# One inference step of a four-layer diffusion trunk: conditioning blocks moved out of the expert stages, permutation gathers, row-half expert blocks

## The reference

```
mod = (silu(cond) @ ada_w[l] + ada_b[l])           # 6 x 1024: shift, scale, gate, twice
h = h + gate1 * mixer(rmsnorm(h) * (1 + scale1) + shift1)
t = rmsnorm(h) * (1 + scale2) + shift2
group = top-1 of 4 by softmax(t @ w_gr + b_gr); experts = top-2 of the group's 4
h = h + gate2 * sum over the two chosen e of w_e * (silu(t @ w_gate[e]) * (t @ w_up[e])) @ w_down[e]
```

## Time and profile before

| what | value |
|---|---|
| median of 3 runs | 1820.84 us (1820.57 to 1822.17) |
| execution that was profiled | 1820.69 us |
| its span, first to last instruction | 1818.9 us |
| TensorE busy | 1723.6 us, 95% |
| VectorE, ScalarE, GpSimd busy | 518.1, 364.6, 99.8 us |
| moved | 614.07 MB, mean 338 GB/s |
| mean granted TensorE clock | 0.973 |

### The profile page before, as it was taken

How to read it: one execution, slowest core, us unless ns; L and a number is a source line. 1 busy time by engine, 2 the same in 40 slices (tenths; PEclk the granted TensorE clock), 3 DMA queues, 4 the chain that set the end, 5 groups by cost and what they waited for, 6 DMA issues and landing times.

```text
span 1818.9 us, 20710 instructions
## 1 busy us (share of the span) xinstructions
PE 1723.6 (95%) x8682; PEld 899.4 (49%) x8682; DVE 518.1 (28%) x1146; ACT 364.6 (20%) x703; POOL 99.8 (5%) x151
## 2 busy tenths in 40 slices
PE   5999999999999999999999999999999999799995
PEld 2554344467545434334864443435786644434441
DVE  1130221220442122130022222215234982312123
ACT  2121010121232101021202210112322651201111
POOL 0000000000000000000000000000002950000000
PEclk8989999999899999999999999999999999899998
DMA  9999999999349999998545999998864576599993
GB/s 401 312 424 426 424 423 425 422 378 346 118 156 427 425 423 426 423 382 342 208 185 208 426 424 426 423 424 318 322 229 153 154 229 235 208 426 424 427 422 132
DMA packets 109073, 614.07 MB, mean 338 GB/s; under 512 B 16721, under 2 KB 16865, under 8 KB 60465
## 3 DMA queue, kind: packets, MB, share of 16 engines
q1 hardware_dynamic: 102032, 585.73, 79.5%
q0 software_dynamic: 6944, 26.96, 4.6%
HBM read 608.34 MB, written 4.33 MB: 337 GB/s over the span
## 4 chain that ended last, share of the span: by engine, by line
PE 82%; DVE 5%; DMA 5%; ACT 2%; issue 2%; SPq 2%; POOL 0%; DVEq 0%; POOLq 0%; ACTq 0%
PE psum L1082 23%; PE psum L604 14%; PE psum L597 12%; PE psum L1116 11%; PE psum L1064 6%; PE psum L1133 5%; PE psum L663 4%; DMA ring<-in_moe_w_up 2%; SPq L422 1%; DMA acc<-in_moe_w_up 1%; DVE arena L1803 1%; PE psum L701 1%; DMA ring<-in_fnet_w_o 1%; PE psum L1102 1%; ACT arena L1414 1%
## 5 line engine op out<-in xcount | busy, mean ns | idle before, releaser
L1082 PE MATMUL psum<-ring,arena 128*64 128x512 f32 x1152 | 343.4, 594 | 3.5 <-DMA acc<-in_moe_w_up 2.0
L597 PE MATMUL psum<-at,ring 128*128 128x256 f32 x1024 | 223.6, 380 | 0.0
L597 PEld LDWEIGHTS psum<-at,ring 128*128 128x128 f32 x1024 | 193.7, 190 | 28.4 <-issue 1.6
L1082 PEld LDWEIGHTS psum<-ring,arena 128*64 128x64 f32 x1152 | 108.5, 137 | 168.4 <-issue 168.4
L1082 PE MATMUL psum<-arena 128*64 128x512 f32 x608 | 190.0, 594 | 0.0
L1875 DVE TENSOR_TENSOR outtmp<-psum,gate 128x512 f32<-128x512 f32 x128 | 87.6, 684 | 323.7 <-PE psum L1133 323.7
L604 PE MATMUL psum<-ring,at 128*128 128x512 f32 (+1 forms) x416 | 173.5, 572 | 0.4 <-DVE at L1718 0.4
L1116 PE MATMUL psum<-ring,arena 128*64 128x512 f32 x624 | 138.6, 593 | 0.0
L1866 DVE TENSOR_TENSOR arena<-arena,psum 128x512 f32<-128x512 f32 x32 | 33.9, 1059 | 360.9 <-PE psum L1082 360.9
L1064 PE MATMUL psum<-arena,xn 128*128 128x128 f32 x1024 | 126.0, 284 | 6.4 <-issue 6.4
L604 PE MATMUL psum<-ring,arena 128*128 128x512 f32 x288 | 128.4, 604 | 3.0 <-DMA ring<-in_fnet_w_o 3.0
(11 more groups left out here) (254 smaller groups left out, 1550.2 us busy)
## 6 DMA issues: line engine op xcount, KB each, us to landing
ring<-in_ada_w SPq DMA_DIRECT2D x43, 2048.0 KB, 12.6
ring<-in_moe_w_down SPq DMA_DIRECT2D x39, 2048.0 KB, 22.7
ring<-in_moe_w_up SPq DMA_DIRECT2D x38, 2048.0 KB, 15.8
ring<-in_moe_w_gate SPq DMA_DIRECT2D x34, 2048.0 KB, 18.0
arena<-in_moe_w_gate SPq DMA_DIRECT2D x22, 2048.0 KB, 14.8
arena<-in_moe_w_down SPq DMA_DIRECT2D x17, 2048.0 KB, 20.0
arena<-in_moe_w_up SPq DMA_DIRECT2D x16, 2048.0 KB, 19.7
ring<-in_ssd_w_in SPq DMA_DIRECT2D x12, 2048.0 KB, 8.9
```

Of the source, the lines that this page charges most:

```text
L597: last = nc.tensor.matmul(dst, slot(k)[:, c, m * P:(m + 1) * P], src[:, c, :], start=(c == 0), stop=(c == nk - 1))
L1082: last = nc.tensor.matmul(ps[b][e * CAP:(e + 1) * CAP, :], rows, slot_half(k + e, 4, h)[:, c, :], start=(h == 0 and c == 0), stop=(h == 1 ...
```

## The change

- **Round 0 of the next layer** leaves the routing stretches. A1.0 is loaded and multiplied at the start of layer 1, A2.0 behind Q4 and Q5, A3.0 behind I7 and I0. Layer 1's own later rounds move one step later.
- **Layer 0** goes stream by stream as the other layers do. O0 and O1 are issued right behind round 0 of the conditioning. Routers and biases come as contiguous rows into a spare tile and VectorE copies them.
- **Gathers.** Pair x now holds experts x and x+8, of different groups, so a token is in at most one of them. For each stream VectorE completes the one-hot matrix to a permutation (`permutations`), and the gather becomes transposes with it, one bank for each stream. ScalarE copies stream 0's bank, VectorE merges stream 1's over it under a mask (`merged`). Pair 0 keeps the products.
- **Blocks.** G and U blocks now hold half of the rows of both experts, as D's did; `pair_rows` waits for one block at a time and frees it after its half.
- **Order in the expert loop.** The turns of the activations lie between the halves of the down product, the two halves of the gather around the scatter.

```diff
-    return rest[:EARLY], {0: rest[EARLY:4], 1: rest[4:6], 2: rest[6:8]}
+    rest, after = ada_names(n, (1, 2)), ada_names(n + 1, (0,)) if n < 3 else []
+    if n == 1:
+        return [], {0: rest[0:2], 1: rest[2:4], 2: rest[4:6], 3: rest[6:8], 4: after[0:2], 5: after[2:4]}
+    return rest[:3], {0: rest[3:4], 1: rest[4:6], 2: rest[6:8], 3: after[0:2], 4: after[2:4]}
+EVICTED = {1: {1: (1, 1), 3: (1, 2)}, 2: {0: (2, 1), 2: (2, 2), 4: (3, 0)}, 3: {0: (3, 1), 2: (3, 2)}}
+TURNED = {1: {2: (1, 1), 4: (1, 2)}, 2: {1: (2, 1), 3: (2, 2), 5: (3, 0)}, 3: {1: (3, 1), 3: (3, 2)}}
...
-    ada_names(0, (0, 1)) + ["O0", "A0.2.0", "A0.2.1", "O1", "A0.2.2", "A0.2.3"] + ada_names(1, (0,)),
-    mixed(1, [f"Q{j}" for j in range(6)]) + ["O0", "O1"] + ada_names(2, (0,)),
-    mixed(2, [f"I{j}" for j in V_FIRST]) + [f"O{j}" for j in range(4)] + ada_names(3, (0,)),
+    ada_names(0, (0, 1)) + ["A0.2.0", "A0.2.1", "A0.2.2", "O0", "A0.2.3", "O1"],
+    ada_names(1, (0,)) + mixed(1, [f"Q{j}" for j in range(6)]) + ["O0", "O1"],
+    mixed(2, [f"I{j}" for j in V_FIRST]) + [f"O{j}" for j in range(4)],
...
+def issued(n):
+    if n == 0:
+        return ada_names(0, (0,)) + ["O0", "O1"] + ada_names(0, (1, 2)) + MOE
+    if n == 1:
+        return MIX[1] + ["U0.0", "U0.1", "G0.0", "G0.1"] + MOE[4:]
+    return MIX[n] + MOE
...
+            first_up = n == 1 and w in ("U0.0", "U0.1")
+            if n == 0 or expert and not first_up:
...
-                if k == AT[0, "O0"]:
-                    sp.dma_start(wr[:, :, :, 0:EG], a["wgr"]).then_inc(consts_in, 16)
...
+                if k == AT[0, "A0.2.0"]:
+                    sp.dma_start(routers[:, 0, 0:128], a["wgr"].rearrange("p l c e -> p (l c e)")).then_inc(consts_in, 16)
...
+                    half = rows.rearrange("p (e x) c n -> p x e c n", e=2)[:, x, :, c * e:c * e + c, :]
+                    if ROOM[k] == RING + 2:
...
+                        load(k, rooms[ROOM[k]].rearrange("p (e c n) -> p e c n", e=2, c=c), half)
...
+            def first_map():
+                map_part(0, 0, 0, 0, ft, 1)
+                ada_slot(0, "A0.2.0")
+                map_part(0, 0, 1, 0, ft, 1)
+                ada_turned(0, 1)
+                ada_slot(0, "A0.2.1")
+                ada_slot(0, "A0.2.2")
+                map_part(0, 1, 0, 0, ft, 1)
+                ada_slot(0, "A0.2.3")
+                stream_turned(0, 1, 0)
+                for half in range(2):
+                    last = dense_tok(AT[0, "O1"], 1, ps[out_bank(0, 1, 1)][:, :], ft, half * DC // 2, DC // 2,
+                                     half == 0, half == 1, wc0=half * DC // 2)
+                    if half == 0:
+                        ada_turned(0, 2)
+                last.then_inc(slot_done, 1)
...
+                    if n == 1:
+                        if s == 0:
+                            ada_slot(1, "A1.0.3")
+                        else:
+                            ada_turned(1, 0)
...
                     ada_turned(0, 0)
+                elif n == 1:
+                    for q in range(3):
+                        ada_slot(1, f"A1.0.{q}")
                 else:
...
@@ -808,6 +823,7 @@
                         for c in range(4):
                             last = nc.tensor.transpose(bank(4 + h, 4, P)[:, c, :], kT[:, 4 * h + c, 0:P], mat("ident"))
                         last.then_inc(kt_mm, 1)
...
+                            pe.wait_ge(mod_ready, 3 * (n + 1) + 1)
                         if i >= 3:
...
-                    stream_logits(n, 0)
-                    stream_logits(n, 1)
-                    stream_folded(n, 0)
-                    stream_folded(n, 1)
-                    stream_tokens(n, 0)
-                    stream_tokens(n, 1)
-                    for q in range(QUARTERS):
-                        ada_slot(n, f"A1.0.{q}")
-                else:
-                    stream_logits(n, 0)
-                    if n < 3:
-                        for q in range(2):
-                            ada_slot(n, f"A{n + 1}.0.{q}")
-                    stream_folded(n, 0)
-                    stream_turned(n, 1, 1)
-                    stream_tokens(n, 0)
-                    stream_logits(n, 1)
-                    stream_folded(n, 1)
-                    stream_tokens(n, 1)
-                    if n < 3:
-                        for q in range(2, QUARTERS):
-                            ada_slot(n, f"A{n + 1}.0.{q}")
...
+                nc.tensor.matmul(of_pos[:, 3, :], mat("ones"), sel16[:, 0, :], start=True, stop=False)
+                nc.tensor.matmul(of_pos[:, 3, :], mat("ones"), sel16[:, 1, :], start=False, stop=True).then_inc(pos_mm, 1)
...
+                def gather(x, t):
+                    pe.wait_ge(onehot_ready, PAIRS * n + x + 1)
                     for s in range(S):
-                        last = nc.tensor.transpose(bank(3, S, P)[:, s, :], onehot_w[:, s, :], mat("ident"))
-                    last.then_inc(gt_mm, 1)
+                        if s:
+                            pe.wait_ge(xg_merged, MERGES * n + 2 * (x - 1) + t)
+                            if x == 1:
+                                pe.wait_ge(xg_ev, 2 * PAIRS * n + 2)
+                        else:
+                            pe.wait_ge(xg_ev, 2 * (PAIRS * n + x) + t)
+                        for cc in range(4):
+                            c = 4 * t + cc
+                            last = nc.tensor.transpose(bank(4 + s, 4, P)[:, cc, :], xn[:, s, c * P:(c + 1) * P], onehot[:, s, :])
+                        last.then_inc(xg_mm, 1)
+                    if t:
...
                 def pair_rows(x, w, b):
-                    k = AT[n, f"{w}{x}.0"]
-                    arrive(k)
-                    arrive(k + 1)
                     for h in range(2):
-                        pe.wait_ge(xg_ev, 2 * (PAIRS * n + x) + h + 1)
+                        k = AT[n, f"{w}{x}.{h}"]
+                        arrive(k)
+                        if x:
+                            pe.wait_ge(xg_merged, MERGES * n + 2 * (x - 1) + h + 1)
...
+                            pe.wait_ge(xg_ev, 2 * PAIRS * n + h + 1)
...
-                def down_product(x):
...
+                        if h and between is not None:
+                            act_transposes(between)
...
-                        down_product(x - 1)
+                        down_product(x - 1, x)
+                        if x < LAST:
+                            gather(x + 1, 0)
+                        scatter(x - 1)
                     else:
-                        if n < 3:
-                            ada_turned(n + 1, 0)
-                        gather(1)
-                    act_transposes(x)
-                    if 0 < x < LAST:
-                        gather(x + 1)
-                    if x:
-                        scatter(x - 1)
+                        gather(1, 0)
+                        act_transposes(0)
+                    if x < LAST:
+                        gather(x + 1, 1)
...
+            def permutations(n):
...
+                kept, count, before = q(0), q(1), q(2)
+                link(V.tensor_scalar(taken[:, 1:S + 1, :], posr[:, S:S + 2, :], float(CAP), None, ALU.min))
+                link(V.tensor_scalar(before, posr[:, 0:S, :], float(CAP), None, ALU.min))
...
+            def merged(n, x, t):
+                if t == 0:
+                    starts = taken[:, 1, :].rearrange("p (e x) -> p e x", e=2)[:, :, x:x + 1].to_broadcast([P, 2, CAP])
+                    link(V.tensor_tensor(of_late[:, :, :], mats[:, MAT_AT["iota"], 0:CAP].unsqueeze(1).to_broadcast([P, 2, CAP]), starts, ALU.is_ge))
+                dve.wait_ge(xg_mm, (GATHERS + 2) * n + 2 + 4 * (x - 1) + 2 * t + 2)
+                dve.wait_ge(xg_ev, 2 * (PAIRS * n + x) + t + 1)
+                V.copy_predicated(xg[:, x % 2, 4 * t:4 * t + 4, :],
+                                  of_late[:, :, :].rearrange("p e j -> p (e j)").unsqueeze(1).to_broadcast([P, 4, P]),
+                                  bank(5, 4, P)).then_inc(xg_merged, 1)
...
                 for x in range(PAIRS):
                     activated(x)
-                    if x == 0 and n < 3:
-                        modulation(n + 1, 0)
+                    if x < LAST:
+                        merged(n, x + 1, 0)
                     if x:
-                        for i in range(4):
+                        for i in range(3):
                             add_rows(x - 1, i)
+                    if x < LAST:
+                        merged(n, x + 1, 1)
+                    if x:
+                        add_rows(x - 1, 3)
                     if x + 2 < PAIRS:
                         build_onehot(n, x + 2)
```

More of the change, by code:

```diff
@@ L93 @@
 LAST = PAIRS - 1
-def first_issued(n):
-    return {0: [], 1: ["A2.0.0", "A2.0.1", "G0.0", "G0.1", "A2.0.2", "A2.0.3"],
-            2: ["G0.0", "G0.1", "A3.0.0", "A3.0.1", "A3.0.2", "A3.0.3"], 3: ["G0.0", "G0.1"]}[n]
-ISSUE = []
-for _n in range(DEPTH):
-    _early = first_issued(_n)
-    for _w in MIX[_n] + MOE:
```

(64 more changed lines are left out.)

213 lines of the change are left out of this document (122 added, 91 removed).

## The result

The changed kernel takes 1831.1 us (median of 5 runs, 1830.12 to 1832.46), the kernel before 1820.84 beside it: ratio 1.0053, 95% interval 1.0042 to 1.0064. It is slower by some 10 us, where the sum forecast no change at 1822 and the stated range ended at 1831. The execution profiled took 1830.44, its span is 1828.7, 9.8 more than before. TensorE is busy 1696.8 us, 26.8 less than before, and the span is longer.

The account below looks back on a forecast made before the run. Transfers were taken to bound the expert stages (TensorE by a hair in layer 3), TensorE the dense ones. Opening -7.7, stages -28.8, entrance +8.4, moved slots +22.3, routing +6.6, waits 0.5 gave +1.3: 1822 us, range 1811 to 1831.

Parts of the forecast that it names:

- forecast case: Whole kernel: all terms as summed, 1822 us, own range 1815 to 1829; chance 50%.
- rival 3: Layer 1's entrance: Q0 lands later than 28.5 after the last down block, clock low; 8 us more, 1830; 20%.
- named signs of being wrong: Stages of 213 or more, products waiting on VectorE, first Q product over 31 after last landing, TensorE gaps between Q blocks.
- Opening: Layer 0 up to its experts: first gate product at 128 against 135.7, -7.7 us (bounds -3 and -11).
- Expert stages: First gate to last down start 210.4 in all four, -28.8 together; includes 0.5 for smaller runs, bounds nothing to 2.
- TensorE's floor: Expert stages: TensorE alone would need 204 us, gathers saving 1.7 in 7 of 8 pairs; 6.4 cover to 210.4.
- Layer 1's entrance: Layer 0's last landing to first Q product: 28.5 plus 2 for the clock, against 23.0 now; +8.4 in the sum.
- Moved slots and routing: Stretches before the expert stages: moved slots with rows and turn +22.3, routing with its product in layers 1 to 3 +6.6.
- Rival 1: Routing in layers 1 and 2, and Q0: the clock stays up, total -7, 1815; 14%.
- Rival 2: Dense stages: the moved slots do not cost because they fill waits, up to -22, 1800; 8%.
- rival 4: Expert stages: gather's merge on VectorE delays TensorE over 0.9 us a pair, each further 1 us costs 28; 1850; 4%.
- Rival 5: Expert stages: waits for late blocks make the clock fall there too, 2.6 us a stage, 1832; 4%.

Follow-up runs that it names:

- strided: Changed kernel with router weights and biases loaded straight into their strided tiles, without VectorE copies: 1840.93 us, ratio 1.0104 to the kernel before.
- whole: Changed kernel with gate and up blocks of one whole expert each instead of row halves of both: 1838.58 us, ratio 1.0091 to the kernel before.
- back23: Changed kernel with round 0 of layers 2 and 3 back in the routing stretches, layer 1's still moved: 1816.65 us, ratio 0.9968 to the kernel before.
- halfslots: Changed kernel with half of TensorE's passes in the moved slots of layers 2 and 3, all bytes loaded: 1823.58 us, ratio 1.0006.
- latetables: Changed kernel with GpSimd's loads of attention's tables (2 MB) held until layer 1's last round 0 slot is multiplied: 1829.05 us, ratio 1.0037.
- back123: Changed kernel with round 0 of layers 1, 2 and 3 back in the routing stretches: 1805.73 us, ratio 0.9906 to the kernel before.
- split3: back123 with two of A3.0's four blocks multiplied behind I7 in layer 2's dense stretch instead: 1805.32 us, ratio 0.9911 to the kernel before.
- products: Changed kernel with all gathers as one-hot products, without turns, merges or permutation: 1848.97 us, ratio 1.0145 to the kernel before.
- nogather: Changed kernel with the gathers of pairs 2 to 7 left out in each layer: 1830.06 us, ratio 1.0037 to the kernel before.
- backprod: back123 with product gathers as well: 1817.81 us, ratio 0.9978 to the kernel before.

## Why the prediction was right or wrong

The mechanism held: stages bound by landings at 211 to 213 in all layers, landings in the chain, dense stretches that pay the moved work in full, transfers at rest in front of each stage (7 to 12 us without a landing, not 15). The number did not: the sizes of single terms were off, nearly all to one side, 8.6 us in the span. The 1831.1 lies outside the forecast case's own 1815 to 1829 and at the very edge of the range. That it comes so near rival 3's 1830 is luck: that rival's condition came true, its price did not, and most of the excess arose elsewhere. Two of the named signs of being wrong showed: a stage of 213.3, in layer 3, and a first Q product 32.2 after the last landing, past the 31. The cases' chances add up to 30, 30 and 40 in a hundred for faster, same and slower; how they became 0.28, 0.35 and 0.37 is not said.

- **Opening**: -7.7 predicted, -8.0 measured. strided shows that the contiguous routers carry it, with 10.4.
- **Expert stages**, the step that failed most: -28.8 predicted, -23.8 measured. The term that was mis-sized is the 0.5 for smaller runs. whole shows the row halves worth 1.7 to 2.9 a stage and not 3.0. The 3.5 is there: the first block behind a stage's start lands 11.7 after it in layers 0, 1 and 3 and 13.6 in layer 2, instead of 15.2. But gate and up blocks then land 4.97 apart and not 4.90, which takes 2 us back, the upper bound that I had given. In layer 3, where the 207.5 was read, the last landing is at 213.0 and not 211.4, by just this; in layers 0 to 2, where no final norm's gain is loaded in between, it is at 212.0, 211.7 and 212.3. In layer 3 also 1.14 of issue stands in front of the last down product: 213.3 measured, 210.4 predicted. The same stage takes 212.1 or 212.2 in back23, halfslots, latetables and strided and 213.7 and 213.8 in back123 and split3; what makes that difference is not shown.
- **TensorE's floor**: 204 predicted, 207.6 by products, since a turned gather saves 1.2 a pair and not 1.7. It changed nothing here, nogather shows it; the cover was 3 us and not 6.4.
- **Layer 1's entrance**: +8.4 predicted with 2 for the clock; +9.9 to the first Q product and 1.55 more in it. That is rival 3's place, and its condition came true: Q0 landed 32.1 after the last down block, past the 28.5. But its price was not 8: latetables takes Q0's landing out of the chain and gains nothing that can be told, since the scaling ends at 30.3 anyway and the low clock takes back 1.1 of the 1.8. What I had too small was the chain up to Q0's start: with Q0's landing out of it, it took 30.4 where I had 28.5 before the 2 for the clock. Q0's product lost 2.7 to the clock there, and 1.55 in the changed kernel.
- **Moved slots and routing**: in layer 1 +17.7 predicted, +19.5 measured with the 1.55 of Q0's clock in it, so 17.9; in layer 2 +11.3 predicted, +12.2 measured. halfslots confirms that it is mostly TensorE's time.
- **Rival 1** (the clock stays up) is refuted, and back123 points the other way: slots in the routing stretch help to keep it up. Without slots the gather took 6.21 and 6.39 in layers 1 and 2 of the changed kernel, with slots 3.81 each in back123. They do not keep it up always. I had weighed one stretch of three without a drop and held its slots against it, but the other two of the kernel before have slots too, and dropped in part. Its chain of waits, layers 0 and 2:

```profile
130.03 5.44 PE psum L1064 x32
...
1007.95 5.41 PE psum L1064 x32
```

  Over all profiles here the last 20 us before a stage have a mean granted clock of 0.79 to 1.00 where four slots lie in the routing, and of 0.54 to 0.74 where none do. The gather itself, one point in that stretch, took 3.81 to 6.69 with slots and 5.33 to 6.70 without.
- **Rival 2** falls with halfslots and back23, **rival 4** with nogather. **Rival 5** falls too: windows of the changed kernel over the last pairs of layers 0 to 2, where TensorE is idle for 3.4 to 4.3 us of 40, mostly in waits of 0.9 to 1.2 us for landings, have a granted clock of 1.00:

```profile
300.00:339.00 39.00, 35.65 (x156) 13.72 (x158) 10.19 (x16) 5.31 (x8) 0.00 (x0) 1.00 1.01 421
745.00:785.00 40.00, 35.96 (x158) 13.62 (x154) 9.90 (x15) 5.31 (x8) 0.00 (x0) 1.00 1.01 420
1203.00:1242.00 39.00, 34.69 (x153) 13.61 (x154) 9.18 (x14) 5.31 (x8) 0.00 (x0) 1.00 1.01 422
```

The Trainium skill's "TensorE: Matmul & The Clock Gate", section "HAM oscillation — how this bites in real kernels", has a loop that waits for a transfer in each step start every step cold. Its waits are about 3 to 5 us each, so it is not this case, and the prediction should not have called rival 5 the likelier by it; these windows show no cold start after waits of up to 1.2 us. The cold starts of this kernel are at Q0 and behind routing, with 1.55 and about 2.5 us lost at each.

What the prediction did not ask is what the rest of the change is worth without the move. It credited full rooms to the move as pure gain: 5.3 and 3.9 a stage by back23, against stretches longer by 8.9 and 12.5. All that gained came from the other parts: back123 has them alone and beats both kernels, at 1805.73. The change's 10 us of loss are 26 lost by the move and 16 gained by the rest.

The traces say where the rest gains. back123's span is 12.6 under that of the kernel before, and 10.7 of it is layer 0's opening (124.97 for 135.69) and 2.2 layer 3's stage; the stages of layers 0 to 2 are as long as before (220.6, 217.4, 216.5 for 220.9, 216.8, 216.8). So of turned gathers, row halves and the new loop order together little is left there. With product gathers (backprod) the stages of layers 1 to 3 are 2.2 longer each than in the kernel before, so the turns make up for what the new loop costs. The loop order was not undone by itself.

## What to carry to other kernels

Where a stage is bound by transfers and its neighbour by TensorE, compare the two sums over the whole stage, blocks in hand included, and not a pair against a pair. Work that fills the latency of a serial chain such as routing costs little of TensorE's time where it stands and helps to keep the clock up; its blocks here left rooms empty, 4 to 9.5 us a stage. Moved to a full engine it cost its length and the clock it held, 9 to 29 us a stretch. When blocks are cut into shorter runs to free rooms sooner, price the lower rate over the whole stage: it took 2 of 3.5 us back. Undo each part of a bundled change by itself: this one hid a gain of 0.9% behind a loss.

## What was not expected of the hardware

- 2 MB blocks in runs of 8 KB a partition land 4.97 us apart, in runs of 16 KB 4.90; 421 against 426 GB/s in layer 1's stage (changed kernel, whole).
- Counted from layer 0's last landing, Q0's product started 1.8 us sooner in latetables and ended only 0.7 sooner: it took 16.70 for 15.56, more of it at the low clock.
- Issuing one load of 262 KB (128 partitions by 512 numbers) into a strided tile held SyncE 23.92 us; in contiguous rows, line 432 of the changed kernel, 1.82. All four router and bias loads together took 28.6 us of SyncE (35.61 to 64.22) and 10.5 (35.36 to 45.81).
